# Where the gate product of a retrieved expert is made, and when two heads of the second tile are routed

## What is computed

```python
q = (xt @ w_q).reshape(PEER_BLOCK, PEER_HEADS, 2, PEER_DK // 2)
s = jnp.einsum('thcd,hcnd->thcn', q, keys)
sv, si = lax.top_k(s, PEER_TOPK)
...
top_s, top_p = lax.top_k(cand_s, PEER_TOPK)
idx = jnp.take_along_axis(cand_i, top_p, axis=-1)
g = jax.nn.softmax(top_s, axis=-1)
a = jnp.einsum('td,thkd->thk', xt, u_tab[idx])
hk = (g * jax.nn.gelu(a, approximate=False)).astype(xt.dtype)
return jnp.einsum('thk,thkd->td', hk, v_tab[idx])
```

## Time and profile before

| | us |
|---|---|
| median of 3 runs (lowest, highest) | 3215.26 (3214.26, 3216.42) |
| the profiled execution | 3215.45 |
| its span, first to last instruction | 3213.5 |
| PE busy in the span | 2480.3 (77%) |
| DVE busy | 2302.1 (72%) |
| ACT busy | 1710.0 (53%) |
| the gather queue's packets, share of 16 DMA engines | 84.7% |
| bytes moved by all queues | 1255.97 MB, mean 391 GB/s |

### The profile page before, as it was taken

How to read it: one execution, slowest core, us unless ns; L and a number is a source line. 1 busy time by engine, 2 the same in 40 slices (tenths; PEclk the granted TensorE clock), 3 DMA queues, 4 the chain that set the end, 5 groups by cost and what they waited for, 6 DMA issues and landing times.

```text
span 3213.5 us, 41527 instructions
## 1 busy us (share of the span) xinstructions
PE 2480.3 (77%) x13984; PEld 2082.5 (65%) x13984; DVE 2302.1 (72%) x6345; ACT 1710.0 (53%) x2524; POOL 1218.9 (38%) x1095
## 2 busy tenths in 40 slices
PE   8986889766987878876877787878687665686878
PEld 6655778655676767765766666766576555576665
DVE  2737666886567887778956777677668888678655
ACT  1325456776455754445545685444555555456773
POOL 1113333334433434433433344334344444434441
PEclk9888989977988888997987799999799777678899
DMA  7568999989999999999999899999999999989997
GB/s 294 192 251 359 410 409 383 411 328 390 411 421 420 400 421 421 421 421 396 393 421 421 335 420 414 421 421 421 411 421 421 402 421 418 412 351 421 421 421 288
DMA packets 182531, 1255.97 MB, mean 391 GB/s; under 512 B 21358, under 2 KB 26222, under 8 KB 33584
## 3 DMA queue, kind: packets, MB, share of 16 engines
q0 software_dynamic: 156320, 1113.83, 84.7%
q1 hardware_dynamic: 24416, 136.35, 10.6%
q10 hardware_dynamic: 1584, 3.15, 0.3%
HBM read 1246.78 MB, written 6.50 MB: 390 GB/s over the span
## 4 chain that ended last, share of the span: by engine, by line
DMA 35%; PE 25%; DVE 23%; ACT 7%; DVEq 4%; issue 4%; POOL 1%; SPq 0%; ACTq 0%; POOLq 0%
DMA arena<-in_uv,idx 34%; DVE arena L1655 10%; PE acc L1909 8%; ACT arena L1173 5%; PE bank L1936 5%; PE bank L1927 4%; PE bank L1714 2%; PE acc L1906 2%; DVEq L1561 2%; DMA panel<-in_panels 1%; PE bank L1748 1%; POOL arena L986 1%; ACT L1163 1%; DVE ya L1504 1%; DVE yb L1534 1%
## 5 line engine op out<-in xcount | busy, mean ns | idle before, releaser
L986 POOL DMA_INDIRECT arena<-in_uv,idx x1024 | 1174.0, 1146 | 1758.5 <-PE acc L1909 1522.7
L1909 PE MATMUL acc<-cst,arena 128*128 128x128 f32 x8128 | 1256.7, 317 | 673.0 <-ACT arena L1173 671.3
L1173 ACT ACTIVATE arena<-arena,act_w 128x1024 f32<-128x1024 f32 x1032 | 1129.0, 1141 | 1023.8 <-DVE act_w L1664 1006.9
L1909 PEld LDWEIGHTS acc<-cst,arena 128*128 128x128 f32 x8128 | 1099.4, 164 | 851.8 <-ACT arena L1173 822.1
L1655 DVE CUSTOM_DVE_ANT_0 arena<-arena,h 128x1024 f32<-128x1024 f32 x1024 | 1247.4, 1221 | 450.2 <-DMA arena<-in_uv,idx 431.9
L1936 PE MATMUL bank<-hT,panel 128*128 128x264 f32 (+2 forms) x1856 | 421.7, 382 | 2.3 <-DMA panel<-in_panels 1.3
L1936 PEld LDWEIGHTS bank<-hT,panel 128*128 128x128 f32 x1856 | 344.5, 196 | 51.4 <-issue 2.3
L1163 ACT ACTIVATE act_w<-dots 128x2 f32<-128x2 f32 x520 | 101.6, 195 | 87.8 <-DVE dots L1655 80.5
L1163 ACT ACT_TABLE_LOAD x109 | 139.8, 1283 | 2.0
L1714 PE MATMUL bank<-hT,panel 128*128 128x264 f32 (+1 forms) x512 | 120.4, 394 | 13.5 <-DMA panel<-in_panels 13.5
L1664 DVE TENSOR_TENSOR act_w<-act_w,gate 128x2 f32<-128x2 f32 x512 | 80.5, 157 | 58.0 <-ACT act_w L1163 56.3
(11 more groups left out here) (236 smaller groups left out, 2327.2 us busy)
## 6 DMA issues: line engine op xcount, KB each, us to landing
panel<-in_panels SPq DMA_DIRECT2D x116, 1024.0 KB
arena<-in_uv,idx POOLq DMA_INDIRECT x1024
arena<-in_cache_k POOLq DMA_DIRECT2D x16, 512.0 KB, 6.4
arena<-in_cache_v POOLq DMA_DIRECT2D x16, 512.0 KB, 4.9
arena<-out_y_s POOLq DMA_DIRECT2D x8, 512.0 KB, 9.1
arena<-in_panels SPq DMA_DIRECT2D x4, 1024.0 KB, 8.0
h<-in_h SPq DMA_DIRECT2D x2, 1024.0 KB
out_y_p<-h SPq DMA_DIRECT2D x3, 512.0 KB
```

What stands on the lines that cost most here:

```text
L986: nc.gpsimd.indirect_dma_start(uv[:, slot_of(e), :], None, uv_dram[layer], bass.IndirectOffsetOnAxis(ids[:, r:r + 1], 0)).then_inc(gathere ...
L1173: nc.scalar.activation(row, row, ACT.Copy, scale=act_w[:, 1, half, r:r + 1]).then_inc(weighted, 1)
L1909: m = mm(acc[:, c * P:(c + 1) * P], row, const("ident"), is_transpose=True, start=False, stop=True, skip_group_check=True)
```

## The change

Two things are changed.

First, the product of Gelu and gate moves from DVE to ACT. At the first pair of each group of eight experts ACT copies the eight gates into `act_w[:, 0]`, after a wait for them (`gates_ready`, a new semaphore that DVE raises in `gates`). For each pair it then does the Gelu of two dots, a drain, two activations of one column with the gate as scale, a drain, and the two v rows. The rows of a pair now follow its own Gelu at once. `two_weights` on DVE is gone, with the semaphore that told ACT of it; the two dots of a pair follow each other.

Second, the lanes of routing: tile 0's last 13 pieces are done in units 12 to 18 rather than 12 to 20, tile 1's first 25 pieces (six heads) in units 18 to 32 rather than the first 17 in 20 to 32, and its last 8 (two heads) rather than 16 in units 0 to 10 of window 1.

```diff
--- before.py
+++ after.py
@@ -433,12 +433,12 @@
         others = self.others()
         r1, r2 = self.route(0, 1), self.route(0, 2)
         first_window((0, 1, [r[6]]), (1, 2, [r[7]]), (1, 6, n1 + t1 + q[0:2] + r[8:12]), (6, 13, q[2:] + late), (7, 12, r[12:20]),
-                     (12, 20, r[20:]), (20, 32, r1[:17]), (15, 29, others))
+                     (12, 18, r[20:]), (18, 32, r1[:25]), (15, 29, others))
         bg = self.mix(0, 1)
         self.at_panel[bg[0].panel] = "rows"
         bg += self.norm(0, GROUP_TILES[1], False) + self.turn(GROUP_TILES[1], self.ln_of, "norm") + self.features("pq", 0, 1)
         self.last_other_mix = [x for x in bg if x.kind == "mix"][-1]
-        window(0, 1, (0, 10, r1[17:]), (14, 30, bg), (24, 32, r2[:13]))
+        window(0, 1, (0, 10, r1[25:]), (14, 30, bg), (24, 32, r2[:13]))
         lots = steps[1][3] + steps[2][3]
         for j in range(HEADS):
             for b, at in ((2, 36 + 7 * (j // 2) + 3 * (j % 2)), (3, 64 + 2 * j)):
@@ -625,7 +625,7 @@
         sums = sb("sums", [P, 2, HEADS])
         cst = sb("cst", [P, N_CONST])
         dots = sb("dots", [P, 2, GROUP])
-        act_w = sb("act_w", [P, 2, 2, GROUP])
+        act_w = sb("act_w", [P, 3, 2, GROUP])
         small = sb("small", [P, 72])
         state = sb("state", [P, C, 2, NS])
         cw = sb("cw", [P, 3, C])
@@ -788,7 +788,7 @@
         top_ready = sem("top_ready")
         gexp_done = sem("gate_exps")
         idx_done = sem("expert_ids")
-        gated = sem("weights_of_two_experts_ready")
+        g_done = sem("gates_ready")
         gathered = [sem(f"gathered{r}") for r in range(SLOTS_UV)]
         dot_done = sem("dots_done")
         gelu_done = sem("gelu_done")
@@ -1156,30 +1156,31 @@
                         nc.scalar.activation(r_exs[u % 2], r_tvs[u % 2], ACT.Exp, bias=r_nms[u % 2],
                                              accum_out=r_sums[u % 2]).then_inc(gexp_done, 1)
 
-            def two_gelus(G, q):
+            def two_experts(G, q):
 
                 half, s = G % 2, slice(2 * q, 2 * q + 2)
                 act.wait_ge(dot_done, G * GROUP + 2 * q + 2)
-                nc.scalar.activation(act_w[:, 0, half, s], dots[:, half, s], ACT.Gelu).then_inc(gelu_done, 1)
-
-            def two_rows(G, q):
-
-                half = G % 2
-                act.wait_ge(gated, G * 4 + q + 1)
+                nc.scalar.activation(act_w[:, 1, half, s], dots[:, half, s], ACT.Gelu).then_inc(gelu_done, 1)
+                act.drain()
+                for r in range(2 * q, 2 * q + 2):
+                    nc.scalar.activation(act_w[:, 2, half, r:r + 1], act_w[:, 1, half, r:r + 1], ACT.Copy,
+                                         scale=act_w[:, 0, half, r:r + 1])
+                act.drain()
                 for r in range(2 * q, 2 * q + 2):
                     e = G * GROUP + r
                     if e < FIRST_BY_ROWS:
                         row = uv[:, slot_of(e), D:2 * D]
-                        nc.scalar.activation(row, row, ACT.Copy, scale=act_w[:, 1, half, r:r + 1]).then_inc(weighted, 1)
+                        nc.scalar.activation(row, row, ACT.Copy, scale=act_w[:, 2, half, r:r + 1]).then_inc(weighted, 1)
                         continue
                     if e >= FIRST_BY_ROWS + DIAGS:
                         act.wait_ge(slot_done, e - DIAGS + 1)
                     nc.scalar.activation(diag[:, r % DIAGS, :], const("ident"), ACT.Copy,
-                                         scale=act_w[:, 1, half, r:r + 1]).then_inc(weighted, 1)
+                                         scale=act_w[:, 2, half, r:r + 1]).then_inc(weighted, 1)
                 if G * GROUP + 2 * q == FIRST_BY_ROWS:
                     act.wait_ge(slot_done, FIRST_BY_ROWS)
                     nc.scalar.activation(yb[:], acc[:], ACT.Copy).then_inc(turned_over, 1)
 
+            gates5 = gate[:].rearrange("p b h (a r) -> p b h a r", a=2)
             later = []
             for kind, layer, b, lots in steps:
                 if kind == "alone":
@@ -1193,10 +1194,13 @@
                     if len(later) > BEHIND:
                         for x in later.pop(0):
                             background(x)
-                    if t > 0:
-                        two_rows(first_group(layer, b) + (t - 1) // 4, (t - 1) % 4)
-                    two_gelus(G, q)
-                two_rows(G, q)
+                    if q == 0 and b < TB:
+                        act.wait_ge(g_done, place(layer, b) * HEADS + hd + 1)
+                        nc.scalar.activation(act_w[:, 0, G % 2, :], gates5[:, b, hd, t // 4 % 2, :], ACT.Copy)
+                    elif q == 0:
+                        act.wait_ge(ixs_ready, layer + 1)
+                        nc.scalar.activation(act_w[:, 0, G % 2, :], gs8, ACT.Copy)
+                    two_experts(G, q)
                 for lot in later:
                     for x in lot:
                         background(x)
@@ -1551,7 +1555,7 @@
                 dve.wait_ge(gexp_done, unit + 1)
                 V.reciprocal(r_inv, r_sums[unit % 2])
                 dve.drain()
-                V.tensor_scalar(gate[:, b, hd, :], r_exs[unit % 2], r_inv, None, ALU.mult)
+                V.tensor_scalar(gate[:, b, hd, :], r_exs[unit % 2], r_inv, None, ALU.mult).then_inc(g_done, 1)
 
             def background(x):
 
@@ -1646,22 +1650,14 @@
                             for back in (1, 0):
                                 gates(x.b, x.hd - back, x.u - back)
 
-            def dot(e, x_rows):
-
-                G, r = e // GROUP, e % GROUP
-                dve.wait_ge(gathered[slot_of(e)], 16 * (use_of(e) + 1))
-                if r == 0:
-                    dve.wait_ge(gelu_done, G * 4 + 4)
-                V.tensor_tensor_reduce(uv[:, slot_of(e), 0:D], uv[:, slot_of(e), 0:D], x_rows, 1.0, 0.0, ALU.mult, ALU.add,
-                                       dots[:, G % 2, r:r + 1]).then_inc(dot_done, 1)
-
-            def two_weights(layer, b, t):
-
-                G, q = first_group(layer, b) + t // 4, t % 4
-                s = slice(2 * q, 2 * q + 2)
-                dve.wait_ge(gelu_done, SEED_GELU + G * 4 + q + 1)
-                of = gate[:, b, t // 8, t % 8 * 2:t % 8 * 2 + 2] if b < TB else gs8[:, s]
-                V.tensor_tensor(act_w[:, 1, G % 2, s], act_w[:, 0, G % 2, s], of, ALU.mult).then_inc(gated, 1)
+            def two_dots(G, q, x_rows):
+                for r in range(2 * q, 2 * q + 2):
+                    e = G * GROUP + r
+                    dve.wait_ge(gathered[slot_of(e)], 16 * (use_of(e) + 1))
+                    if r == 0:
+                        dve.wait_ge(gelu_done, G * 4 + 4)
+                    V.tensor_tensor_reduce(uv[:, slot_of(e), 0:D], uv[:, slot_of(e), 0:D], x_rows, 1.0, 0.0, ALU.mult, ALU.add,
+                                           dots[:, G % 2, r:r + 1]).then_inc(dot_done, 1)
 
             later = []
             for kind, layer, b, lots in steps:
@@ -1678,12 +1674,7 @@
                             background(x)
                     if t == 0:
                         dve.drain()
-                    x_rows = h[:, b, :] if b < TB else x_sample[:]
-                    dot(G * GROUP + 2 * q, x_rows)
-                    if t > 0:
-                        two_weights(layer, b, t - 1)
-                    dot(G * GROUP + 2 * q + 1, x_rows)
-                two_weights(layer, b, t)
+                    two_dots(G, q, h[:, b, :] if b < TB else x_sample[:])
 
 
         @block.tensor
```

## The result

| | before | with the change |
|---|---|---|
| median of the runs, us | 3214.26 (5 runs) | 3198.08 (5 runs, 3190.78 to 3199.22) |
| ratio, 95% interval | | 0.9947 [0.9931, 0.9963] |
| the same two, measured once more, us | 3216.71 (9 runs) | 3193.69 (5 runs) |
| ratio, 95% interval | | 0.9926 [0.9912, 0.9939] |
| the profiled execution, us | 3215.45 | 3193.24 |

The change makes the kernel faster by 17 to 24 us (0.53% and 0.74%); the two profiled executions stand 22.2 apart. The forecast was 32 us. Sign and range were right; the forecast's gain was 1.3 to 1.9 times what came.

The account below looks back on a forecast made before the run. The DMA link, at most 421 GB/s, was taken as the bound, with 84 us to win where engines, mostly DVE, held it up. The terms summed to -32 us, from 3215.45 to 3183; range 3150 to 3208.

Parts of the forecast that it names:

- The products leave DVE: In the DVE-bound stretches, DVE saves 0.07 us for each of 520 products, of which 2.5 us counts.
- The rows no longer wait for DVE: Slots held 3 us less: 3 us won from 1050, 1500 and 1775 each, 2 in smaller stretches, 8 in the first tile.
- the term of the first tile: From 275 to 640 us, with 8 slots, a shorter hold of each slot wins 8 of 17.2 us.
- rival B: The 10 us won from 640 are lost again in the first tile: -15 us, 3200; chance 0.14.
- DVE no longer waits at the end of a window: After the sample tiles DVE goes on without ACT's Gelu: 5 us won from 1775, 3 from 2825.
- Two heads routed earlier: 19 us of DVE work moves from the stretch at 640 to the first tile: 10 us won, 3 lost.
- ACT's new work: 0.65 us a pair on ACT, mostly hidden, but 1 us lost from 1075 and 3 from 1825.
- The remainder: All smaller stretches together win 2 us by the shorter hold; the last pair's drained products add 0.5 us.
- A: With a shorter hold nearly all the idle link is won but some: about -60 us, 3155; chance 0.15.
- C: The wait is nearly all hidden behind full transfers, so nothing counts: about -2 us, 3213; chance 0.09.
- D: ACT becomes the bound, its added work paid in some 110 pairs: +50 us, 3265; chance 0.07.

Follow-up runs that it names:

- e2: The kernel before with only the new lanes of routing, the product still on DVE: 3207.81 us, ratio 0.9977 to the kernel before.
- e3: The changed kernel with each pair's rows put back behind ACT's other work of the next pair, product still on ACT: 3193.05 us, ratio 0.9929.
- e1: The changed kernel with the lanes of routing as before, so only the product moved to ACT: 3202.20 us, ratio 0.9954.
- e4: The changed kernel with DVE made to wait for the previous pair's Gelu between the two dots of each pair: 3202.34 us, ratio 0.9952.
- e11: The changed kernel with PE adding only four of the eight column parts of each sample expert: 3189.42 us, ratio 0.9910.
- e5: The changed kernel with each pair's two products on ACT made a second time, into a place nothing reads: 3209.47 us, ratio 0.9960.
- e12: The changed kernel with one gather less in flight from expert 219 on: 3202.93 us, ratio 0.9957.

## Why the prediction was right and wrong

**The products leave DVE, -2.5.** Too small to be told apart in the whole. In the DVE-bound experts 416 to 448, 16 pairs, DVE is busy 77.7 us where it was 78.9, near the 16 x 0.07 = 1.1 us of the working, and the stretch takes 1.3 us less; the product's versions all take 89.5 to 90.2 us there, before and e2 91.1 and 91.0.

**The rows no longer wait for DVE, -3, -3, -3, -2 and -8 in the first tile.** This is the step that failed: the term of the first tile above all. The 3 us off the chain came (3.01 us in the pair shown, dot to row 6.8 to 3.8), but "a slot as held 3 us less", with "about one gather more in flight", did not follow: the hold stayed at 31 us, and e3, which takes over half of the saving back in the first tile and nearly all of it behind that, is as fast. In its place the runs show this. From 1050, where -3 was forecast, -3.9 came, from the product part (e1 has it, e2 has 1.3 of it); e3 has it too, but keeps most of the shorter chain there, so whether it is the chain or the freed DVE stays open. From 1500, where DVE is the bound, 1 us came rather than 3. In the first tile nothing came of 8. The rows stood ready sooner and PE, busy 309 of 387 us, took them later; its waits for rows, 74.7 us before, are still 70.2. What those stand behind was not taken apart. The prediction had PE's part in hand, since it named PE's 144 of 165 us there, and used it against rival B but not against its own term.

**DVE no longer waits at the end of a window, -5 and -3.** Right behind the first sample tile: -5 us of idle link there in all (e1, without the routing: -3.5), of which e4, with the wait put back, lacks 2.4 to 3.4 us; that this place scatters by 3 us leaves the sign shown and the size not. Wrong in sign behind the second: +3. DVE's wait for gathers there, kernel after, 2810 to 2875 us:

```profile
DVE arena L1659 <- DMA arena<-in_uv,idx: 15.8, 9, 4.7
```

Before, it waited 15.7 us for ACT in its place. DVE was set free 15.7 us sooner and met slots whose gathers had not come, because PE had not yet freed them: the wait changed its name. The prediction had said that PE is the bound there and still took 3. That the link idles 3 us *more* has to do with PE as well. Ahead of the sample tile's sums PE does thirty small products; here from the first of them to the first of the sums, before and with the change:

```profile
2824.25:2833.01 8.76, 7.67 (x30) 3.87 (x30) 8.05 (x26) 6.26 (x9) 1.21 (x2) 0.74 1.00 417
...
2802.12:2812.83 10.71, 10.64 (x30) 5.97 (x30) 8.35 (x24) 9.03 (x18) 0.39 (x1) 0.54 0.77 321
```

The same thirty take PE 10.64 us for 7.67, at a granted clock of 0.54 for 0.74 (means over the stretch: with the change PE is nearly always at the lower of its two levels, 1.2 rather than 2.4 GHz), and the last sum of the sample tile ends 43.5 us after dot 904 where it was 41.3. Every version with the product on ACT shows that end later (42.9 to 45.0 us, but for e11), e2 as before (41.3). In e4 26 of the thirty take as long as before, 5.2 us, and PE waits 3.6 us for ACT rather than 2.2. So it comes with the product on ACT; why PE's clock is lower there in most of them stays open.

**Two heads routed earlier, -10 and +3.** Right: e2 won 10.2 us on the experts 128 to 176 (8.2 of idle link) and lost at most 2.2 in the first tile. The 24 pairs take 5.7 us each in the change, which is the forecast's figure. But DVE, which the prediction expected still near 90%, is at 73% (100.9 of 137.4 us), and ACT, at 121.0 of 137.4, is near 90%.

**ACT's new work, +1 and +3.** The price of a pair was right (0.63 for 0.65 us). The stretch from 1825 to 1900, kernel after:

```profile
1825.00:1900.00 75.00, 65.29 (x395) 49.79 (x394) 57.68 (x158) 72.01 (x111) 34.75 (x30) 0.98 1.01 418
```

ACT is busy 96% of it, as forecast, and the link moves 418 GB/s where it moved 410: no loss of 3 us is to be seen. The cost is elsewhere: by e5 it is some 7 to 19 us in all and more than half of it in the experts 128 to 176, so the term of 4 us was low and its places were not those named, though the 5.7 us a pair of the routing's term had allowed for ACT there.

**The remainder, -2 + 0.5.** Too small: -5 came, mostly in the experts 712 to 904 and 936 to 1039 (12.1 us idle before, 8.5 after). Two of these losses, in 176 to 256 and 712 to 808, are the ones that grow in e12.

**The rivals.** A (3155) is out: the link still idles 84 to 86 of 108 us. B (3200) is half right, as told; by its time alone it is nearer to both measurements than the forecast (3183), and only the traces speak against it, since the 10 us from 640 were not lost again in the first tile. That the forecast's range held is thus no proof of its sum: the 8 us of the first tile and the 3 behind the second sample tile did not come, and 2 to 3 us more than said came in the small losses. C (3213) lies outside both measurements. D is out by e5 and by the time itself. The rule of the Trainium skill (ScalarE: Activation LUTs, Rules for kernel authors), by which such a multiplication belongs on VectorE, holds by busy time: 0.48 us for two on ACT against 0.157 on DVE. In this kernel the trace speaks against following it, since what counts is not the 0.3 us but who must wait for whom, and the product on ACT made the kernel 13 to 15 us faster (e1). And by the 358 GB/s that the Trainium skill (DMA: Bandwidth & Descriptors, Where 436 GB/s comes from) gives as a core's bound, the experts 520 to 568, at 371 GB/s before, had nothing to win; they went to 386, and took 5.8 us less.

## What to carry to other kernels

In a ring of slots, the time that a shorter chain saves can go straight into the next wait, as it did here; look first at who takes the result next, and whether that engine was idle. When an engine is freed from a wait, read what it will meet there: behind the first sample tile DVE met landed gathers and up to 5 us were won, behind the second it met empty slots and none were. A small operation that links two engines may be cheaper on the slower engine that needs its result, if the faster one must otherwise stand in line. And when work is added to an engine, look for the stretch in which it is already near full with work that others wait for: a mean price hides that more than half was paid in one place.

## What was not expected of the hardware

- Two activations of one column, each with a pointer for its scale, take 0.48 us back to back, with a group mean of 287 ns, hardly less than the root of one column (294 ns); the doubles of e5 average 279. A drain between such small activations costs under 0.1 us (the Gelu ends at 700.19, the product starts at 700.27).
- ACT at 96% over the 75 us from 1825 left the link at 418 GB/s, while in the experts 128 to 176, at 88 to 90%, 9 us more of ACT's busy time cost 6. A share of busy time did not tell the two apart.
- In the same thirty products PE's granted clock was 0.74 before and 0.54 with the change, though no instruction of PE's had been changed.
- The same kernel gave 0.9947 [0.9931, 0.9963] in one series and 0.9926 [0.9912, 0.9939] in another, with medians 4.4 us apart. Terms of 1 to 3 us, which most of the prediction's were, cannot be tested one by one against such a measure; the idle link by experts, which repeats to 1 to 3 us a place, serves better. Part of the scatter stands ahead of the first dot, which comes at 243.4 to 252.9 us with the same work before it.
